# Where the gate of a convolution module is computed: GpSimd and ScalarE before, one VectorE pass in the middle of another chunk's taps after

## The chip, the cores and the metric

The kernel runs on one core of a Trainium2 chip. The metric is the device time of one execution in microseconds (us), lower is better. Engines are named as the profile names them: PE (TensorE, the matmuls; PEld its weight loads), DVE (VectorE), ACT (ScalarE), POOL (GpSimd) and SP (SyncE, which here only issues DMAs).

## What is computed

The reference is a two-layer backbone over 1024 latent and 256 context tokens of width 1024. Layer 0 mixes tokens with a Conformer convolution module, layer 1 with a gated linear attention; each is followed by a mixture of experts. The change touches one step of layer 0's convolution module:

```python
def conv_module(h, pw1_w, pw1_b, dw_w, dw_b, ln_g, ln_b, pw2_w, pw2_b):
    a, g = jnp.split(h @ pw1_w + pw1_b, 2, axis=-1)
    u = a * jax.nn.sigmoid(g)
    u = lax.conv_general_dilated(u, dw_w[:, None, :], ...) + dw_b   # 31 taps per channel
    u = jax.nn.silu(layernorm(u, ln_g, ln_b))
    return u @ pw2_w + pw2_b
```

## The kernel before

The program runs stage after stage, with a barrier of all engines between two. The stage in question is `conv_taps`. It holds the normalised input transposed (`ht`, channels on partitions, in two fp32r halves `hi` and `lo`, so that one fp32 product is three matmuls, lines 98 to 100) and works on eight chunks of 128 output channels; chunk number 2i + b uses buffer b of the pair i. In this document the chunks are counted 0 to 7. Per chunk:

- SP loads the chunk's weights (`raw`, line 427); ACT rounds them to `w.hi` (`high`, line 563); POOL computes the rest, `w.lo` (`low`, line 469, 128x2048). `w` is a single buffer, so `high` waits until the previous chunk's products are done.
- PE computes the two halves of pw1, `za` (for a) and `zg` (for g), in three groups of columns of 256, 512 and 512 (`CONV_GROUPS`: the context tokens, then the latent ones), a group at a time. There is one PSUM buffer for each group of each half, so PE's next chunk waits, group by group, until the last one was read.
- Behind each chunk PE computes some columns of the modulation vectors (`units`, line 541): three units behind a chunk of buffer 0, two behind one of buffer 1. Their weights come by DMA (line 438), ACT takes the sum (line 574), POOL adds the bias (line 490, 2x512) and stores it by DMA (line 493).
- The gate u = (za + bias) * sigmoid(zg + bias): ACT writes sg = sigmoid (line 587) and copies za + bias to `u` in SBUF (line 589), POOL multiplies `u` by `sg` in place (line 477), one operation for each group and engine.
- DVE computes the 31 taps over 1295 columns: two `tensor_scalar` (lines 631 and 633) and 29 `scalar_tensor_tensor` (line 638), alternately into `acc[0]` and `acc[1]`, then their sum (line 642), after a small copy of the next chunk's per-channel scalars (line 613). It waits for the three `u_ready` of its chunk before the first tap.

The order on each engine is written out by hand and every queue is in order. The lines that make the waits around the gate are these, PE's before each group and ACT's before its chunk:

```python
516                     for g, (t0, n, _) in enumerate(CONV_GROUPS):
518                         if not (first and b == 0):
519                             pe.wait_ge(s(f"a_ready{g}{1 - b}"), i + b)
```

POOL's order is low, units' output, gate for each chunk. The stage ends when DVE's last sum is done; then the barrier and the stage of the second product (`pw_...` in the profile) follow.

Of the kernel before, what the change touches and what calls it, by code (L numbers as in the profile page):

```python
# [385 lines left out]
ADA_UNITS = [(0, 0, 2, 0, 2 * D), (0, 0, 2, 1, 2 * D), (0, 1, 3, 0, 0), (1, 1, 3, 1, 0), (1, 1, 3, 2, 0)]  # L386


def conv_taps(nc, d, ht, vt, vecs, cs):

    with ExitStack() as ctx:
# [20 lines left out]
        with nc.Block() as block:  # L414
# [47 lines left out]
            @block.gpsimd  # L462
            def _(pool):
                for b in range(2):
                    pool.memset(u[b][:, :], 0.0).then_inc(s("u_zero"), 1)

                def low(b, i):
                    pool.wait_ge(s(f"w_hi{b}"), i + 1)
                    pool.tensor_tensor(w.lo[:, :, :, :], raw[b][:, :, :, :], w.hi[:, :, :, :].bitcast(F32),
                                       ALU.subtract).then_inc(s(f"w_lo{b}"), 1)  # L470

                def gate(b, i):

                    for g, (t0, n, c0) in enumerate(CONV_GROUPS):
                        pool.wait_ge(s(f"sig_ready{g}{b}"), i + 1)
                        pool.wait_ge(s(f"a_ready{g}{b}"), i + 1)
                        pool.tensor_tensor(u[b][:, c0:c0 + n], u[b][:, c0:c0 + n], sg[g][:, 0:n], ALU.mult)\
                            .then_inc(s(f"u_ready{g}{b}"), 1)

                def units_out(b, i, first):  # L480

                    for j, (when, l, per, at, c0) in enumerate(ADA_UNITS):
                        if when != b:
                            continue
                        u = i * len(ADA_UNITS) + j
                        pool.wait_ge(s("ada_b_loaded"), (u + 1) * 16)
                        pool.wait_ge(s("ada_taken"), u + 1)
                        if not (first and j == 0):
                            pool.wait_ge(s("stored"), u * 16)
                        pool.tensor_tensor(ada_row[:, :], ada_sum[:, :], ada_b[:, :], ALU.add)\  # L490
                            .then_inc(s("ada_out"), 1)
                        pool.wait_ge(s("ada_out"), u + 1)
                        pool.dma_start(d.mods[l].rearrange("s m n -> s (m n)")[:, ds((i * per + at) * N + c0, N)],
                                       ada_row[:, :]).then_inc(s("stored"), 16)

                low(0, 0)
                gate(0, 0)
                low(1, 0)
                units_out(0, 0, True)
                gate(1, 0)  # L500
                with pool.Fori(1, pairs) as i:
                    low(0, i)
                    units_out(1, i - 1, False)
                    gate(0, i)
                    low(1, i)
                    units_out(0, i, False)
                    gate(1, i)
                units_out(1, pairs - 1, False)
                pool.wait_ge(s("stored"), 16 * pairs * len(ADA_UNITS))

            @block.tensor
            def _(pe):
                pe.wait_ge(s("rows_loaded"), 96)
                for k in range(KC):
                    last = pe.transpose(pv[:, k, :], rows[:, k * P:(k + 1) * P], ident[0:VEC_ROWS, 0:VEC_ROWS])
                last.then_inc(s("pv_ready"), 1)

                def chunk(b, i, first):
                    pe.wait_ge(s(f"w_lo{b}"), i + 1)
                    for g, (t0, n, _) in enumerate(CONV_GROUPS):  # L520

                        if not (first and b == 0):
                            pe.wait_ge(s(f"a_ready{g}{1 - b}"), i + b)
                        for h, z in ((1, zg[g]), (0, za[g])):
                            for k in range(KC):
                                last = product3(pe, z[:, 0:n], w.hi[:, k, h, :], w.lo[:, k, h, :],
                                                ht.hi[:, k, t0:t0 + n], ht.lo[:, k, t0:t0 + n], k == 0, k == KC - 1)
                        last.then_inc(s(f"z_ready{g}{b}"), 1)

                def units(b, i, first):  # L530
                    for j, unit in enumerate(ADA_UNITS):
                        if unit[0] != b:
                            continue
                        u = i * len(ADA_UNITS) + j
                        if not (first and j == 0):

                            pe.wait_ge(s("ada_taken"), u)
                        for h in range(2):
                            pe.wait_ge(s(f"ada_loaded{h}"), (u + 1) * 16)
                            for k in range(KC // 2):  # L540
                                last = pe.matmul(ada_acc[0:2, :], cs[:, h * (KC // 2) + k, :], ada_w[h][:, k, :],  # L541
                                                 start=h == 0 and k == 0, stop=h == 1 and k == KC // 2 - 1)
                            last.then_inc(s(f"ada_used{h}"), 1)

                for b in range(2):
                    chunk(b, 0, True)
                    units(b, 0, True)
                with pe.Fori(1, pairs) as i:
                    for b in range(2):
                        chunk(b, i, False)  # L550
                        units(b, i, False)

            @block.scalar
            def _(act):
                act.preload_act_table(ACT.Sigmoid)
                act.wait_ge(s("u_zero"), 2)

                def high(b, i, first):
                    act.wait_ge(s(f"w_loaded{b}"), i * 32 + 32)
# [16 lines left out]
                def chunk(b, i, first):  # L576

                    act.wait_ge(s(f"vec_ready{b}"), i + 1)
                    if not first:

                        act.wait_ge(s("taps_summed"), i * 2 + (b - 1))
                    for g, (t0, n, c0) in enumerate(CONV_GROUPS):
                        act.wait_ge(s(f"z_ready{g}{b}"), i + 1)
                        if not (first and b == 0):

                            act.wait_ge(s(f"u_ready{g}{1 - b}"), i + b)
                        act.activation(sg[g][:, 0:n], zg[g][:, 0:n], ACT.Sigmoid, bias=vec[b][:, V_BG:V_BG + 1])\
                            .then_inc(s(f"sig_ready{g}{b}"), 1)
                        act.activation(u[b][:, c0:c0 + n], za[g][:, 0:n], ACT.Identity, bias=vec[b][:, V_BA:V_BA + 1])\
                            .then_inc(s(f"a_ready{g}{b}"), 1)  # L590

                high(0, 0, True)
                chunk(0, 0, True)
# [13 lines left out]
            def _(dve):  # L607
# [4 lines left out]
                def vector(b, i):  # L612
                    dve.tensor_copy(vec[b][:, :], vecs[:, ds(i * 2 + b, 1), :].rearrange("p o v -> p (o v)"))\
                        .then_inc(s(f"vec_ready{b}"), 1)

                def chunk(b, i, first=False, last=False):
                    n = i + 1

                    if b == 0:
                        vector(1, i)  # L620
                    elif not last:
                        vector(0, i + 1)
                    dve.wait_ge(s(f"vec_ready{b}"), n)
                    for g in range(3):
                        dve.wait_ge(s(f"u_ready{g}{b}"), n)
                    if not (first and b == 0):

                        dve.wait_ge(s("taps_summed"), i * 2 + b)


                    dve.tensor_scalar(acc[0][:, :], u[b][:, 0:CONV_OUT], vec[b][:, 0:1], vec[b][:, V_DWB:V_DWB + 1],
                                      ALU.mult, ALU.add).then_inc(s(f"tap0{b}"), 1)
                    dve.tensor_scalar(acc[1][:, :], u[b][:, 1:1 + CONV_OUT], vec[b][:, 1:2], None, ALU.mult)\
                        .then_inc(s(f"tap1{b}"), 1)
                    for k in range(2, TAPS):
                        q = k % 2
                        dve.wait_ge(s(f"tap{q}{b}"), i * len(range(q, TAPS, 2)) + k // 2)
                        dve.scalar_tensor_tensor(acc[q][:, :], u[b][:, k:k + CONV_OUT], vec[b][:, k:k + 1],  # L638
                                                 acc[q][:, :], ALU.mult, ALU.add).then_inc(s(f"tap{q}{b}"), 1)
                    for q in range(2):  # L640
                        dve.wait_ge(s(f"tap{q}{b}"), n * len(range(q, TAPS, 2)))
                    dve.tensor_tensor(vt[:, ds(i * 2 + b, 1), :].rearrange("p o n -> p (o n)"), acc[0][:, :],
                                      acc[1][:, :], ALU.add).then_inc(s("taps_summed"), 1)

                vector(0, 0)
                for b in range(2):
                    chunk(b, 0, first=True)
                with dve.Fori(1, pairs - 1) as i:
# [1895 lines left out]
```

## Time and profile before

| | us |
|---|---|
| median of 3 runs | 3388.13 |
| lowest and highest | 3384.37, 3390.13 |
| the profiled execution | 3385.44 |
| its span in the trace | 3383.8 |
| DVE, PE, ACT, POOL busy in the whole span | 2113.4, 2720.6, 1407.5, 509.8 |
| the taps stage, first load to last sum | about 118 to 605 |

The whole-program shares mix stages with different limits: PE is the busiest engine over the span, but in the stage that is changed another engine is. The stage has therefore to be read by itself, with the windows that are cut at its own borders, and then the timelines of the engines in it, which list instructions in order of time with the idle time in front of them and what ended it.

### The profile page before, as it was taken

To read this page: it belongs to the slowest core of one execution; us is meant where nothing else is said; L and a number is where in the kernel's file an instruction comes from. 1 tells how busy PE (TensorE), PEld (TensorE's weight loads), DVE (VectorE), ACT (ScalarE), POOL (GpSimd) and SP (SyncE) were. 2 spreads that over 40 slices of the span, in tenths; PEclk is the share of its full clock that TensorE was granted. 3 is DMA by queue.
4 is the path that set the end of the run, shared out by engine and by line. 5 is a ranking of instruction groups with operands and counts; after the bars stand their busy time and mean duration, and the time that the engine had idled before them with its cause. 6 is when DMAs were issued, how large, how long until landed. Compare 5 with 4: busy or idle time off the path is not lost. (4 is left out here: it accounts for less than half of the span.)

```text
span 3383.8 us, 39400 instructions
## 1 busy us (share of the span) xinstructions
PE 2720.6 (80%) x12298; PEld 2063.0 (61%) x12298; DVE 2113.4 (62%) x1769; ACT 1407.5 (42%) x1439; POOL 509.8 (15%) x432
## 2 busy tenths in 40 slices
PE   4598994595399999999925998989775399999980
PEld 1454552484278888888824886766464278888860
DVE  2399999455476777588444002346464488888865
ACT  1211110443166666577323113323232177777752
POOL 0136331100001010011051000022100010110104
PEclk7699997796599999999956999979887599999995
DMA  8243440224188988799564111022354299999965
GB/s 296 90 150 100 137 137 25 94 75 171 48 312 319 332 322 320 276 364 389 210 247 148 72 47 45 13 77 94 111 219 153 100 372 389 390 385 388 395 264 214
DMA packets 296869, 701.09 MB, mean 207 GB/s; under 512 B 22000, under 2 KB 49136, under 8 KB 296774
## 3 DMA queue, kind: packets, MB, share of 16 engines
q1 hardware_dynamic: 256538, 562.40, 46.4%
q0 software_dynamic: 24320, 83.98, 7.0%
q10 hardware_dynamic: 15936, 53.75, 4.2%
q8 instruction: 42, 0.69, 0.1%
q14 instruction: 33, 0.27, 0.0%
HBM read 610.05 MB, written 91.06 MB: 207 GB/s over the span
## 5 line engine op out<-in xcount | busy, mean ns | idle before, releaser
L1379 DVE TENSOR_TENSOR moe_w_lo<-moe_w_raw,moe_w_hi 128x2048 fp32r<-128x2048 f32 x384 | 862.0, 2286 | 83.8 <-ACT moe_w_hi L1308 47.3
L1308 ACT ACTIVATE moe_w_hi<-moe_w_raw 128x2048 fp32r<-128x2048 f32 x384 | 714.0, 1908 | 57.0 <-issue 36.7
L638 DVE SCALAR_TENSOR_TENSOR taps_acc<-taps_u,taps_vec,taps_acc 128x1295 f32<-128x1295 f32 x232 | 382.9, 1725 | 0.0
L98 PE MATMUL moe_pg<-moe_w_hi,moe_xt_hi 128*128 128x512 f32 x592 | 243.7, 412 | 11.3 <-DVE moe_xt_lo L1390 5.9
L98 PE MATMUL moe_py<-moe_w_hi,moe_at_hi 128*128 128x512 f32 x592 | 241.7, 408 | 11.9 <-DVE moe_w_lo L1379 8.2
L99 PE MATMUL moe_pg<-moe_w_lo,moe_xt_hi 128*128 128x512 f32 x592 | 236.9, 400 | 0.0
L100 PE MATMUL moe_pg<-moe_w_hi,moe_xt_lo 128*128 128x512 f32 x592 | 236.9, 400 | 0.0
L99 PE MATMUL moe_py<-moe_w_lo,moe_at_hi 128*128 128x512 f32 x592 | 235.2, 397 | 0.0
L100 PE MATMUL moe_py<-moe_w_hi,moe_at_lo 128*128 128x512 f32 x592 | 234.7, 396 | 0.0
L100 PE MATMUL moe_pu<-moe_w_hi,moe_xt_lo 128*128 128x512 f32 x592 | 234.3, 396 | 0.0
L98 PE MATMUL moe_pu<-moe_w_hi,moe_xt_hi 128*128 128x512 f32 x592 | 234.1, 396 | 0.0
L99 PE MATMUL moe_pu<-moe_w_lo,moe_xt_hi 128*128 128x512 f32 x592 | 234.1, 396 | 0.0
L1211 POOL COPY moe_idx<-plan_token 128x1 int32 (+1 forms) x76 | 16.0, 210 | 1074.5 <-PE moe_pxt L1249 1074.3
L541 PE MATMUL taps_ada_acc<-taps_ada_w,silu_c 128*2 128x512 f32 x320 | 150.2, 625 | 33.1 <-DMA taps_ada_w<-in_ada_w 33.1
L1425 DVE TENSOR_TENSOR moe_a<-moe_sil,moe_pu 128x512 f32<-128x512 f32 x74 | 50.9, 688 | 180.8 <-issue 114.3
L364 PE MATMUL norm_pt<-norm_ident,norm_h 128*128 128x128 f32 x224 | 55.1, 427 | 119.1 <-DVE norm_h L334 119.1
L1318 ACT ACTIVATE moe_y<-moe_py 128x1024 f32<-128x1024 f32 x74 | 76.0, 1027 | 147.7 <-PE moe_py L100 147.7
L98 PEld LDWEIGHTS moe_pg<-moe_w_hi,moe_xt_hi 128*128 128x128 f32 x592 | 113.5, 192 | 36.4 <-issue 12.5
L1217 POOL DMA_INDIRECT moe_xg<-scratch_experts_in,moe_idx x76 | 116.1, 1527 | 124.4 <-issue 124.4
L2197 DVE SCALAR_TENSOR_TENSOR scan_state<-scan_state,scan_es,scan_pds 128x256 f32<-128x256 f32 x160 | 67.4, 477 | 107.2 <-issue 68.6
L98 PEld LDWEIGHTS moe_py<-moe_w_hi,moe_at_hi 128*128 128x128 f32 x592 | 112.1, 189 | 35.8 <-issue 12.3
L1333 ACT ACTIVATE moe_xt_hi<-moe_pxt 128x1024 fp32r<-128x1024 f32 x74 | 75.9, 1025 | 134.6 <-PE moe_pxt L1249 134.6
(296 smaller groups left out, 5544.1 us busy)
## 6 DMA issues: line engine op xcount, KB each, us to landing
moe_w_raw<-in_moe_w SPq DMA_DIRECT2D x384, 1024.0 KB, 10.3
taps_ada_w<-in_ada_w SPq DMA_DIRECT2D x40, 1024.0 KB, 5.3
scratch_experts_out<-moe_y ACTq DMA_DIRECT2D x57, 512.0 KB, 6.3
norm_x<-scratch_residual SPq DMA_DIRECT2D x28, 512.0 KB, 3.5
scan_v<-scratch_gla_values SPq DMA_DIRECT2D x20, 512.0 KB, 4.6
scratch_experts_in<-norm_h POOLq DMA_DIRECT2D x18, 512.0 KB, 3.3
comb_x<-scratch_residual SPq DMA_DIRECT2D x18, 512.0 KB, 5.5
ada_w<-in_ada_w SPq DMA_DIRECT2D x4, 2048.0 KB, 28.6
```

The costliest lines, as they stand in the source:

```text
L98: pe.matmul(out, xh, wh, start=start, stop=False)
L99: pe.matmul(out, xh, wl, start=False, stop=False)
L100: return pe.matmul(out, xl, wh, start=False, stop=stop)
L364: last = pe.transpose(pt[b][:, k, :], h[b][:, k * P:(k + 1) * P], ident[:, :])
L541: last = pe.matmul(ada_acc[0:2, :], cs[:, h * (KC // 2) + k, :], ada_w[h][:, k, :], start=h == 0 and k == 0, stop=h == 1 and k == KC // 2 - 1)
L638: dve.scalar_tensor_tensor(acc[q][:, :], u[b][:, k:k + CONV_OUT], vec[b][:, k:k + 1], acc[q][:, :], ALU.mult, ALU.add).then_inc(s(f"tap{q} ...
L1217: pool.indirect_dma_start(xg[0:rows, :], None, d.hd[:, :], bass.IndirectOffsetOnAxis(idx[0:rows, :], 0))\
L1308: act.activation(hi[m][:, cut, :], raw[m][p][:, cut, :], ACT.Copy).then_inc(s(f"{m}_hi{h}"), 1)
L1318: act.activation(y[:, :], py[:, :], ACT.Copy).then_inc(s("y_out"), 1)
L1333: act.activation(xt_hi[:, :, :], pxt[:, :, :], ACT.Copy).then_inc(s("xt_hi"), 1)
L1379: dve.tensor_tensor(lo[m][:, cut, :], raw[m][p][:, cut, :], hi[m][:, cut, :].bitcast(F32), ALU.subtract).then_inc(s(f"{m}_lo{h}"), 1)
L2197: last = dve.scalar_tensor_tensor(state[r][:, h, :], state[r][:, h, :], es[r][st.b][:, h, end:end + 1], pds[:, h, :], ALU.mult, ALU.add)
```

## The change

ACT's copy of za to `u` and POOL's product are removed. In their place DVE does one `scalar_tensor_tensor` for each group, (za + bias) * sg, that reads za from PSUM and sg from SBUF and writes `u`. DVE does chunk 0's gate before its first tap. The gate of every later chunk stands between tap 15 and tap 16 of the chunk before it (`GATE_AT = 16`). PE's wait for `a_ready` becomes a wait for `sig_ready` and `u_ready`; ACT's waits for `taps_summed` and for the zeroed `u` go, and the latter is now DVE's.

```diff
+GATE_AT = 16
...
             @block.gpsimd
...
-                def gate(b, i):
-
-                    for g, (t0, n, c0) in enumerate(CONV_GROUPS):
-                        pool.wait_ge(s(f"sig_ready{g}{b}"), i + 1)
-                        pool.wait_ge(s(f"a_ready{g}{b}"), i + 1)
-                        pool.tensor_tensor(u[b][:, c0:c0 + n], u[b][:, c0:c0 + n], sg[g][:, 0:n], ALU.mult)\
-                            .then_inc(s(f"u_ready{g}{b}"), 1)
...
             @block.tensor
...
-                            pe.wait_ge(s(f"a_ready{g}{1 - b}"), i + b)
+                            pe.wait_ge(s(f"sig_ready{g}{1 - b}"), i + b)
+                            pe.wait_ge(s(f"u_ready{g}{1 - b}"), i + b)
...
             @block.scalar
-                act.wait_ge(s("u_zero"), 2)
...
-                    if not first:
-
-                        act.wait_ge(s("taps_summed"), i * 2 + (b - 1))
...
-                        act.activation(u[b][:, c0:c0 + n], za[g][:, 0:n], ACT.Identity, bias=vec[b][:, V_BA:V_BA + 1])\
-                            .then_inc(s(f"a_ready{g}{b}"), 1)
...
             @block.vector
+                def gate(b, i):
+
+                    for g, (t0, n, c0) in enumerate(CONV_GROUPS):
+                        dve.wait_ge(s(f"z_ready{g}{b}"), i + 1)
+                        dve.wait_ge(s(f"sig_ready{g}{b}"), i + 1)
+                        dve.scalar_tensor_tensor(u[b][:, c0:c0 + n], za[g][:, 0:n], vec[b][:, V_BA:V_BA + 1],
+                                                 sg[g][:, 0:n], ALU.add, ALU.mult).then_inc(s(f"u_ready{g}{b}"), 1)
...
                     for k in range(2, TAPS):
                         q = k % 2
+                        if k == GATE_AT:
+                            if b == 0:
+                                dve.wait_ge(s("vec_ready1"), n)
+                                gate(1, i)
+                            elif not last:
+                                dve.wait_ge(s("vec_ready0"), n + 1)
+                                gate(0, i + 1)
...
                 vector(0, 0)
+                dve.wait_ge(s("u_zero"), 2)
+                dve.wait_ge(s("vec_ready0"), 1)
+                gate(0, 0)
```

On DVE, from the stage's first copy to the first chunk's sum (names: `taps_u` is u, `taps_za` the PSUM tile of a, `taps_sg` the sigmoid):

```order
-L609 COPY channel_vectors<-taps_pv 128x288
-L613 COPY taps_vec<-channel_vectors 128x36 x2
-L631 TENSOR_SCALAR taps_acc<-taps_u,taps_vec 128x1295
-L633 TENSOR_SCALAR taps_acc<-taps_u,taps_vec 128x1295
-L638 SCALAR_TENSOR_TENSOR taps_acc<-taps_u,taps_vec,taps_acc 128x1295 x29
...
+L607 SCALAR_TENSOR_TENSOR taps_u<-taps_za,taps_vec,taps_sg 128x256
+L607 SCALAR_TENSOR_TENSOR taps_u<-taps_za,taps_vec,taps_sg 128x512 x2
+L599 COPY taps_vec<-channel_vectors 128x36
+L624 TENSOR_SCALAR taps_acc<-taps_u,taps_vec 128x1295
+L626 TENSOR_SCALAR taps_acc<-taps_u,taps_vec 128x1295
+L638 SCALAR_TENSOR_TENSOR taps_acc<-taps_u,taps_vec,taps_acc 128x1295 x14
+L607 SCALAR_TENSOR_TENSOR taps_u<-taps_za,taps_vec,taps_sg 128x256
+L607 SCALAR_TENSOR_TENSOR taps_u<-taps_za,taps_vec,taps_sg 128x512 x2
+L638 SCALAR_TENSOR_TENSOR taps_acc<-taps_u,taps_vec,taps_acc 128x1295 x15
```

The unbroken run of 29 taps is now one of 14 and one of 15, with the three operations of the next chunk's gate between them; this form stands in chunks 0 to 6, and chunk 7 keeps the 29 in a row.

On POOL, from the zeroing of u to the output of the first units:

```order
-L465 MEMSET taps_u 128x1325 x2
-L469 ISA
-L469 TENSOR_TENSOR taps_w_lo<-taps_raw,taps_w_hi 128x2048
-L477 TENSOR_TENSOR taps_u<-taps_u,taps_sg 128x256
-L477 TENSOR_TENSOR taps_u<-taps_u,taps_sg 128x512 x2
-L469 TENSOR_TENSOR taps_w_lo<-taps_raw,taps_w_hi 128x2048
...
+L468 MEMSET taps_u 128x1325 x2
+L472 ISA
+L472 TENSOR_TENSOR taps_w_lo<-taps_raw,taps_w_hi 128x2048 x2
+L485 TENSOR_TENSOR taps_ada_row<-taps_ada_sum,taps_ada_b 2x512
+L488 DMA scratch_modulation<-taps_ada_row 2x512
```

The three products between the two `low` are gone, and so at each later chunk; the order of what is left is the same.

## Rows read from the trace of the kernel before

**Rows 1.** Busy time by stage: window, length, then the columns of the first line.

```profile
core 0: us, PE busy (x) PEld busy (x) DVE busy (x) ACT busy (x) POOL busy (x), PEclk, DMA share, GB/s
...
170.00:605.00 435.00, 341.06 (x1322) 191.70 (x1320) 432.85 (x262) 46.52 (x69) 152.14 (x68) 0.90 0.33 107
```

**Rows 2.** The same view, cut into DVE's eight chunks: the last one, and the sum.

```profile
558.50:604.70 46.20, 0.00 (x0) 0.00 (x0) 46.09 (x32) 0.00 (x0) 0.00 (x0) 0.50 0.00 0
sum 434.70, PE 341.06 PEld 191.70 DVE 432.85 ACT 46.52 POOL 152.14; mean PE 42.63 PEld 23.96 DVE 54.11 ACT 5.82 POOL 19.02
```

**Rows 3.** DVE's timeline (start, us [idle before]); last, the tap's line, ns min/median/max.

```profile
169.94 0.95 DVE L631 TENSOR_SCALAR taps_acc<-taps_u,taps_vec 128x1295 f32<-128x1295 f32 x1 [39.89 <-POOL taps_u L477]
170.81 5.13 DVE L633 TENSOR_SCALAR taps_acc<-taps_u,taps_vec 128x1295 f32<-128x1295 f32 x1
175.86 47.22 DVE L638 SCALAR_TENSOR_TENSOR taps_acc<-taps_u,taps_vec,taps_acc 128x1295 f32<-128x1295 f32 x29
...
225.81 4.91 DVE L631 TENSOR_SCALAR taps_acc<-taps_u,taps_vec 128x1295 f32<-128x1295 f32 x1 [0.20 <-POOL taps_u L477]
...
560.14 42.94 DVE L638 SCALAR_TENSOR_TENSOR taps_acc<-taps_u,taps_vec,taps_acc 128x1295 f32<-128x1295 f32 x29
...
L638 DVE SCALAR_TENSOR_TENSOR taps_acc<-taps_u,taps_vec,taps_acc x232: 1552/1556/5800, 175.9 to 601.5; 128x1295 f32<-128x1295 f32 x116
```

**Rows 4.** DVE's and POOL's timelines, single operations; then POOL's three lines, ns min/median/max.

```profile
435.18 5.80 DVE L638 SCALAR_TENSOR_TENSOR taps_acc<-taps_u,taps_vec,taps_acc 128x1295 f32<-128x1295 f32 x1
433.85 5.76 POOL L469 TENSOR_TENSOR taps_w_lo<-taps_raw,taps_w_hi 128x2048 fp32r<-128x2048 f32 x1
184.26 2.56 DVE L638 SCALAR_TENSOR_TENSOR taps_acc<-taps_u,taps_vec,taps_acc 128x1295 f32<-128x1295 f32 x1
213.29 2.39 DVE L638 SCALAR_TENSOR_TENSOR taps_acc<-taps_u,taps_vec,taps_acc 128x1295 f32<-128x1295 f32 x1
202.56 1.94 DVE L638 SCALAR_TENSOR_TENSOR taps_acc<-taps_u,taps_vec,taps_acc 128x1295 f32<-128x1295 f32 x1
256.24 21.53 POOL L477 TENSOR_TENSOR taps_u<-taps_u,taps_sg 128x512 f32<-128x512 f32 x1 [10.35 <-ACT taps_u L589]
...
L469 POOL TENSOR_TENSOR taps_w_lo<-taps_raw,taps_w_hi x8: 4492/4654/5758, 133.6 to 477.1; 128x2048 fp32r<-128x2048 f32 x8
...
L490 POOL TENSOR_TENSOR taps_ada_row<-taps_ada_sum,taps_ada_b x20: 1277/2057/2623, 175.2 to 544.9; 2x512 f32<-2x512 f32 x20
...
L477 POOL TENSOR_TENSOR taps_u<-taps_u,taps_sg x24: 639/1492/21532, 146.6 to 529.7; 128x512 f32<-128x512 f32 x16, 128x256 f32<-128x256 f32 x8
```

**Rows 5.** The timelines of ACT, POOL and PE up to chunk 1's last sigmoid.

```profile
167.30 0.69 ACT L587 ACTIVATE taps_sg<-taps_zg,taps_vec 128x512 f32<-128x512 f32 x1 [9.61 <-PE taps_za L100]
167.88 0.68 ACT L589 ACTIVATE taps_u<-taps_za,taps_vec 128x512 f32<-128x512 f32 x1
...
168.70 1.09 POOL L477 TENSOR_TENSOR taps_u<-taps_u,taps_sg 128x512 f32<-128x512 f32 x1 [9.79 <-ACT taps_u L589]
...
167.19 7.03 PE L541 MATMUL taps_ada_acc<-taps_ada_w,silu_c 128*2 128x512 f32 x16
...
185.41 8.72 PE L541 MATMUL taps_ada_acc<-taps_ada_w,silu_c 128*2 128x512 f32 x16 [2.00 <-DMA taps_ada_w<-in_ada_w]
...
221.91 0.69 ACT L587 ACTIVATE taps_sg<-taps_zg,taps_vec 128x512 f32<-128x512 f32 x1 [9.61 <-PE taps_za L100]
```

**Rows 6.** Two DVE lines with an input in PSUM, elsewhere: ns min/median/max.

```profile
L2197 DVE SCALAR_TENSOR_TENSOR scan_state<-scan_state,scan_es,scan_pds x160: 473/476/484, 2226.1 to 2431.7; 128x256 f32<-128x256 f32 x160
...
L1425 DVE TENSOR_TENSOR moe_a<-moe_sil,moe_pu x74: 686/689/690, 948.6 to 3273.0; 128x512 f32<-128x512 f32 x74
```

**Rows 7.** PE's products of chunks 1 and 2, as windows in the columns of rows 1.

```profile
194.06:221.80 27.74, 27.74 (x145) 23.70 (x144) 27.74 (x19) 2.70 (x5) 6.33 (x4) 1.00 0.15 53
238.20:265.50 27.30, 27.30 (x144) 23.36 (x142) 27.30 (x19) 2.47 (x5) 13.08 (x4) 1.00 0.18 65
```

**Rows 8.** PE's timeline: the last of the three units behind chunk 2.

```profile
292.29 9.95 PE L541 MATMUL taps_ada_acc<-taps_ada_w,silu_c 128*2 128x512 f32 x16 [10.50 <-DMA taps_ada_w<-in_ada_w]
```

## The prediction and its working

> **What bounds the kernel now.** The stage borders come first: the windows cut at them show DVE busy 432.85 of 435.00 us between its first tap and the end of the taps stage, PE 341.06, POOL 152.14 and ACT 46.52 [rows 1]. So between 170 and 605 us the kernel goes at DVE's pace, though DVE is far from the busiest engine over the whole program. A barrier follows, so what the stage's end moves by, the program's end moves by; nothing in the later stages is edited.
>
> Next, what one chunk costs DVE. The window of the last chunk, in which POOL does nothing, is 46.2 us; eight of these would be 369.6, while the eight windows sum to 434.7 [rows 2]. The missing 65.1 us are DVE instructions made longer by POOL. A tap alone records 1.556 us, and the 29 undisturbed ones of the last chunk take 42.94, so from start to start it is (42.94 - 1.556) / 28 = 1.478 [rows 3]. Beside POOL's `low` one takes 5.80, beside a bias addition 2.56, beside a 512-column product 2.39 and beside the 256-column one 1.94 [rows 4]. Less 1.556 that is 4.24, 1.00, 0.83 and 0.38 us for each. Of the 65.1, the seven `low` behind the first of eight take 28.8 (three of them hit a `tensor_scalar`: 4.91 against 0.95, 3.96 each [rows 3, 4]) and the twenty bias additions 20.2, which leaves about 16.1 for the gate's 21 products, their stray hits on small operations and the 0.2 us waits in front of a chunk. Counting three products per chunk for seven chunks gives 7 x (0.38 + 2 x 0.83) = 14.3. I take 16.1 and keep 14.3 as the low end.
>
> **The start of the stage.** Before, chunk 0's last gate goes ACT sigmoid to 167.99, ACT copy to 168.56, POOL product to 169.79, first tap at 169.94 [rows 5]. After, DVE reads PSUM itself at about 168.1, beside nothing else, for one operation of 0.69 [rows 6], and the first tap is at about 168.85: **-1.1 us**.
>
> **The gates on DVE.** One gate is three operations with one input in PSUM. The nearest rows are 0.476 us for 256 columns and 0.689 for 512 [rows 6]; less the 0.078 by which records overlap on DVE (1.556 against 1.478), that is 0.40 + 2 x 0.61 = 1.62 us, at most 1.85 with no overlap. I take 1.65, nearest to the back-to-back taps around it. It can't be below the lower figure, since the same operations end no sooner anywhere in the trace. Six gates (chunks 2 to 7) come to **+9.9** (9.7 to 11.1); chunk 0's is in the start above, chunk 1's in the next step. The Trainium skill, "VectorE: DVE Perf Modes", section on the TRN2 errata, gives 120 cycles plus the columns for a PSUM source, 0.39 and 0.66 us here: 1.71 a gate, 10.3 for six, so the sum would grow by 0.4; the trace's records are 0.03 to 0.08 longer than the page's figures.
>
> **The wait in chunk 0.** This is the step that decides. DVE's queue is in order, so the gate of chunk 1, which stands before tap 16 of chunk 0, holds back fifteen taps until PE has made chunk 1's products. When does DVE get there? The 29 taps start at 175.86; fourteen of them at 1.478, plus three bias additions at 1.0 (POOL's `low` has been paid already in the 5.13 of line 633 [rows 3]), reach 199.6; with the earlier start 198.5. When is the gate ready? PE starts chunk 1 at 194.06, directly behind the units, which wait for weights by DMA [rows 5, 7], so nothing that the change frees can start it sooner; its products take 27.7 us [rows 7], ACT's last sigmoid is 221.91 to 222.60 [rows 5]. The last gate operation then runs from 222.7 and tap 16 starts at 223.3. **+24.8 us** between 198.5 and 223.3, of which 1.6 are chunk 1's gate and some 23 idle; the first two groups are done inside that time. Before, DVE waited 0.20 us in front of chunk 1, at 225.81 [rows 3]. The products of chunk 1 had all of chunk 0's taps to hide under, and now have half of them.
>
> **Do later gates wait too?** From tap 16 at 223.3 DVE needs 23.8 us to the end of chunk 0, plus one `low` and two bias additions (6.2): chunk 1's first tap at 253.3. It then costs 46.2 + 1.65 + 4.2 + 2.5 = 54.6 us a chunk on average, and a gate stands 22.4 us plus POOL's hits after a chunk's start. Gate 2 comes at 281 or so; PE's products for it end as now at 265.5 [rows 7]. Three units take 26.9 us where nothing holds them (167.19 to 194.1 [rows 5]), so chunk 3's products run from about 292.5 to 320, and its gate is reached at about 335. Chunk 4's: PE waits for gate 3 (u_ready, about 337), ends 364, gate at 390. From there PE waits for DVE and not the reverse; the smallest margin is 15 us.  So later gates don't wait.
>
> **The sum.** -1.1 (start) + 24.8 (chunk 0's wait and gate 1) + 9.9 (six gates) - 16.1 (POOL's products gone from DVE's way) = **+17.5 us**. Removing ACT's copies (24 at up to 0.68) gives nothing beyond the start: ACT is busy a ninth of the stage. Against the profiled execution's 3385.44 us (span 3383.8, 1.6 lie around it) that gives 3402.9; the median of the three runs lies 2.7 above the profiled one, so the forecast is 3388.1 + 17.5 = 3405.6, or **3406 us**. With the low end for POOL's products and the high end for the gates it is +20.5; with the wait shorter by 2 us, +15.5.
>
> **Rivals.** (1) POOL is held out and PE comes late. One product of POOL's started at 256.24 and took 21.53 us, though an undisturbed one takes 1.09 [rows 4, 5]: DVE's taps passed it one after another until the chunk's end. If a `low` is held like that, its chunk's products begin late; with a margin of 15 us at gate 3 a hold of 21 costs a second stall of about 6 and saves 4.2 of DVE's, a few such make +3 to +12: 3409 to 3418. It did so once before: while POOL was held at 256 to 280, PE's units fell behind, with 10.50 us idle before the last of them [rows 8]. Against it: in the whole stage none of the seven `low` and none of the twenty bias additions was held beyond one tap (their longest records are 5.76 and 2.62 [rows 4]). The Trainium skill, "SBUF — State Buffer", section "Who interferes with whom", calls the port pair that the two share an exclusive lock that whoever starts first holds for its whole instruction, the other waiting. The 5.80 against 5.76 agree, the 21.53 doesn't, since there POOL lost to one tap after another; by the rule alone this rival is nil and the sum stays.
> (2) The other side: faster, because POOL's remaining work falls out of DVE's way. What is left of contention is six `low` (25) and seventeen bias additions (17), 42 us. If DVE, now with fewer interruptions, keeps POOL out as at 256.24 until a gate, whose operations read only one input from SBUF, these costs vanish; beyond 17.5 us saved, that is four `low` and one addition, the kernel is no longer slower, and at most it ends at 3388 + 17.5 - 42 = 3364. The mechanism exists, since DVE's taps beside the product at 256.24 were not stretched; but it has not once struck a `low`.
> (3) The wait isn't there: chunk 1's products start before 194 because POOL's queue is lighter. Then the sum is -1.1 + 1.6 + 9.9 - 16.1 = -5.7, or 3382. For this the units before them would have to end earlier, and their last releaser is a DMA [rows 5], issued after PE frees the buffer. They would have to end 23 us earlier, and nothing in these rows can give that.
> (4) The change does not do what it says: the gate from PSUM runs much slower beside matmuls. At twice the price, 3.3 a gate, it is +10 more: 3416. The row with 74 executions, 686 to 690 ns, stands beside running matmuls [rows 6].
>
> **How the numbers follow.** The forecast has 0.80, rival (1) 0.08, (2) 0.04, (3) 0.02, (4) 0.03, and 0.03 for what I don't see. A difference of 0.2% (6.8 us) is what a measurement of this kernel can tell from none. Slower by more: forecast, (1), (4) and most of the rest, 0.92; within: 0.04, from the mild forms of (2) and (3); faster: 0.04. The range takes the forecast's +15.5 to +20.5, 3 us of the medians' own scatter at either side and the nearer part of (1) and (4): 3398 to 3417.
>
> **What would show it.** In the trace of the changed kernel DVE should idle some 10 us before each of the two 512-column gates of chunk 1 and a little before the 256-column one, 23 in all, released by ACT's sigmoid or PE's za, and nowhere else; the 512-column gates should record about 0.69 us; chunk 7's taps should take 42.94 again; the stage should end at about 622 where it ended at 604.6; ACT should be free of copies and POOL of products, and POOL should stretch DVE's instructions by some 49 us rather than 65 (7 of these ahead of chunk 0's wait, which they only shorten). The forecast is wrong if DVE idles at a later gate, if a `low` records over 10 us, or if the stage is right and later stages moved.

## The result, and the profile after

| | before | after |
|---|---|---|
| median, us (6 runs each) | 3388.33 | 3403.32 |
| lowest and highest | 3384.37, 3390.7 | 3401.92, 3406.23 |
| span of the profiled execution | 3383.8 | 3403.0 |
| taps stage: DVE's first tap to its last sum | 169.94 to 604.63 | 169.86 to 616.94 |

The change makes the kernel slower: the ratio is 1.0046, with a 95% interval from 1.0033 to 1.0059. Of the 15 us, 12.3 are the taps stage, which ends so much later; from the first tap to the last sum it lasts 447.1 us for 434.7. Two windows cut at its borders answer to [rows 1, 2] (columns: window, length, PE, PEld, DVE, ACT and POOL busy, granted clock, DMA):

```profile
169.86:616.94 447.08, 341.05 (x1325) 191.53 (x1323) 423.52 (x283) 36.07 (x48) 134.79 (x47) 0.89 0.31 104
616.94:3403.00 2786.06, 2296.89 (x10674) 1824.95 (x10674) 1627.22 (x1442) 1327.39 (x1318) 341.95 (x353) 0.89 0.61 223
```

DVE was idle for 2 us of the stage before; now it is idle for 23.6. Its timeline says where. It answers to [rows 3]; in brackets stands the idle time ahead of an operation and what ended it.

```profile
169.86 0.95 DVE L624 TENSOR_SCALAR taps_acc<-taps_u,taps_vec 128x1295 f32<-128x1295 f32 x1
170.73 5.20 DVE L626 TENSOR_SCALAR taps_acc<-taps_u,taps_vec 128x1295 f32<-128x1295 f32 x1
175.84 23.91 DVE L638 SCALAR_TENSOR_TENSOR taps_acc<-taps_u,taps_vec,taps_acc 128x1295 f32<-128x1295 f32 x14
201.29 0.48 DVE L607 SCALAR_TENSOR_TENSOR taps_u<-taps_za,taps_vec,taps_sg 128x256 f32<-128x256 f32 x1 [1.54 <-ACT taps_sg L575]
212.34 0.75 DVE L607 SCALAR_TENSOR_TENSOR taps_u<-taps_za,taps_vec,taps_sg 128x512 f32<-128x512 f32 x1 [10.56 <-ACT taps_sg L575]
223.21 0.75 DVE L607 SCALAR_TENSOR_TENSOR taps_u<-taps_za,taps_vec,taps_sg 128x512 f32<-128x512 f32 x1 [10.13 <-ACT taps_sg L575]
223.88 28.55 DVE L638 SCALAR_TENSOR_TENSOR taps_acc<-taps_u,taps_vec,taps_acc 128x1295 f32<-128x1295 f32 x15
...
276.48 1.80 DVE L607 SCALAR_TENSOR_TENSOR taps_u<-taps_za,taps_vec,taps_sg 128x256 f32<-128x256 f32 x3
278.19 27.86 DVE L638 SCALAR_TENSOR_TENSOR taps_acc<-taps_u,taps_vec,taps_acc 128x1295 f32<-128x1295 f32 x15
...
572.46 42.94 DVE L638 SCALAR_TENSOR_TENSOR taps_acc<-taps_u,taps_vec,taps_acc 128x1295 f32<-128x1295 f32 x29
615.43 1.51 DVE L642 TENSOR_TENSOR taps_out<-taps_acc 128x1295 f32<-128x1295 f32 x1
```

The fourteen taps end at 199.75, and then DVE waits three times for ACT's sigmoid of chunk 1: 1.54, 10.56 and 10.13, or 22.2 us. No later gate waits: at 276.48 the three operations follow each other, in 1.71 us from the start of the first to the start of the next tap.

On POOL something else changed. These rows answer to [rows 4], where the longest `low` (then line 469, now 472) was 5.76 and the longest bias addition (then 490, now 485) 2.62:

```profile
268.66 12.27 POOL L472 TENSOR_TENSOR taps_w_lo<-taps_raw,taps_w_hi 128x2048 fp32r<-128x2048 f32 x1 [26.76 <-ACT taps_w_hi L554]
...
328.75 5.80 POOL L472 TENSOR_TENSOR taps_w_lo<-taps_raw,taps_w_hi 128x2048 fp32r<-128x2048 f32 x1 [25.83 <-ACT taps_w_hi L554]
...
478.84 15.08 POOL L472 TENSOR_TENSOR taps_w_lo<-taps_raw,taps_w_hi 128x2048 fp32r<-128x2048 f32 x1 [27.11 <-ACT taps_w_hi L554]
...
546.12 22.14 POOL L485 TENSOR_TENSOR taps_ada_row<-taps_ada_sum,taps_ada_b 2x512 f32<-2x512 f32 x1 [31.70 <-ACT taps_ada_sum L565]
```

A `low` that takes 4.5 us alone is on record for 12 and 15 here; such an operation, which waits on record while DVE's taps pass it, is called held below. The first one ends at 280.93, 2.7 us into the first tap behind the gate, and that tap shows what it cost DVE:

```profile
278.19 4.11 DVE L638 SCALAR_TENSOR_TENSOR taps_acc<-taps_u,taps_vec,taps_acc 128x1295 f32<-128x1295 f32 x1
```

4.11 less 1.56 is 2.55 us, where a `low` before stretched its tap by 4.24.

### The profile page after: what moved, and what is told of

Same layout as the page of the kernel before. It is cut to its first block and busy times, and to the rows that moved or that the text cites. A ratio compares the mean times of both kernels' runs of the same rounds, so it can differ in the third digit from the quotient of the medians.

```text
span 3403.0 us, 39388 instructions
## 1 busy us (share of the span) xinstructions
PE 2721.8 (80%) x12298; PEld 2065.2 (61%) x12298; DVE 2106.0 (62%) x1793; ACT 1396.1 (41%) x1415; POOL 483.8 (14%) x408
## 5 line engine op out<-in xcount | busy, mean ns | idle before, releaser
L98 PE MATMUL moe_pg<-moe_w_hi,moe_xt_hi 128*128 128x512 f32 x592 | 243.7, 412 | 11.4 <-DVE moe_xt_lo L1393 6.2
L98 PEld LDWEIGHTS moe_py<-moe_w_hi,moe_at_hi 128*128 128x128 f32 x592 | 112.2, 190 | 35.8 <-issue 12.3
L98 PE MATMUL glav_acc<-glav_w_hi,ht_next_hi 128*128 128x512 f32 x288 | 115.5, 401 | 19.5 <-DVE glav_w_lo L1754 19.5
L100 PEld LDWEIGHTS moe_pg<-moe_w_hi,moe_xt_lo 128*128 128x128 f32 x592 | 113.2, 191 | 27.4
```

The source lines that it names most:

```text
L98: pe.matmul(out, xh, wh, start=start, stop=False)
L100: return pe.matmul(out, xl, wh, start=False, stop=stop)
```

## The experiments

**Question 1: is the loss chunk 0's wait, and does it go by the gate's place?** Three kernels move `GATE_AT`, and one moves only chunk 0's gate. Each edit up to question 3 is against the changed kernel.

```diff
-GATE_AT = 16
+GATE_AT = 30
```

> The changed kernel with every gate in front of the last tap (tap 30) instead of tap 16. Theory A (the loss is the wait in chunk 0, and its size is the distance between the gate's place and PE's products): fourteen more taps of 1.478 us run before the wait, so the 22.2 us that DVE idled shrink to 2 or 3, chunk 0 ends some 20.7 us earlier, later gates find their products ready, and the taps stage ends at 596 us where the changed kernel has 616.9; the time is 3382 to 3385, some 0.15% faster than the kernel before. Rival B (the place only moves the wait to another gate, since PE can't keep up with an earlier DVE): DVE idles again at gates 2 and 3, the stage ends no earlier than 606, the time is 3392 or more. Rival C (POOL's work is held out for longer, up to 25 us, PE's units fall behind): idle at gates 4 to 7, stage end 600 to 610.

Measured: 3382.01 us, ratio to the kernel before 0.9979 (0.997 to 0.9988); the stage ends at 599.17. DVE waits 0.32 us before chunk 1's last gate operation and nowhere else but 2.31 at gate 5:

```profile
222.26 0.75 DVE L607 SCALAR_TENSOR_TENSOR taps_u<-taps_za,taps_vec,taps_sg 128x512 f32<-128x512 f32 x1 [0.32 <-ACT taps_sg L575]
...
435.95 1.95 DVE L607 SCALAR_TENSOR_TENSOR taps_u<-taps_za,taps_vec,taps_sg 128x256 f32<-128x256 f32 x3 [2.31 <-ACT taps_sg L575]
```

The same pass from PSUM, put where its data is ready, turns 0.46% slower into 0.21% faster than the kernel before. Theory A holds for the size of the loss; rival B is out. C shows in the trace: two bias additions were on record for 36.91 and 36.66 us, and gate 5 waited 2.31 us behind the second. ACT's queue has its next sum of units ahead of chunk 5's sigmoid, and that sum stood until the addition ended at 434.79; the addition for its part got in only when DVE stood still at the gate, from 433.6 on, for want of this sigmoid.

```diff
-GATE_AT = 16
+GATE_AT = 8
```

> The changed kernel with every gate in front of tap 8 instead of tap 16. Theory A: eight taps fewer run before the wait, which grows by 8 x 1.478 = 11.8 us; later gates keep a margin of some 3 us or more. Stage end 628.7, time 3415 (0.8% over the kernel before). If DVE's idle time is given back later the time stays near 3403.

Measured: 3418.37 us, ratio 1.0083 (1.0068 to 1.0099); first tap to last sum 466.1 us against 447.1, so 19.0 more and not 11.8. The idle time at chunk 1's gate grew to 15.62 + 10.56 + 10.13 = 36.3. The rest is `low`: its longest record is 5.58 here, none was held, and each stretched its tap in full, by 4.24 us where five of the changed kernel's took 2.55. So 14.1 more idle, five times 1.69 more for `low`, and 3.5 less for the bias additions (they stretched DVE by 16.9 us in sum, and by 20.4 in the changed kernel) make 19.1 for the 19.0:

```profile
269.71 5.80 DVE L638 SCALAR_TENSOR_TENSOR taps_acc<-taps_u,taps_vec,taps_acc 128x1295 f32<-128x1295 f32 x1
```

```diff
-GATE_AT = 16
+GATE_AT = 24
```

> The changed kernel with every gate in front of tap 24. Theory A: eight more taps ahead of chunk 0's wait, which shrinks by 11.8 us to 10 or so; stage end 605, time 3391. With the held POOL work of theory H a `low` that arrives behind its gate can be held for over 20 us and make PE late, as in the kernel with only chunk 0's gate moved: then 3 to 8 us more, 3394 to 3399.

Measured: 3392.37 us, ratio 1.0006 (0.9997 to 1.0015), first tap to last sum 435.7, 11.4 less than with tap 16 (11.8 expected). `low` was held five times, as at tap 16, but always ahead of its gate, so PE was not late.

```diff
-                        if k == GATE_AT:
+                        if k == (30 if first and b == 0 else GATE_AT):
```

> The changed kernel with the gate in chunk 0 alone in front of tap 30; all others stay in front of tap 16. Theory A: the wait in chunk 0 shrinks to 2 or 3 us and chunk 1 starts 20.7 us earlier, at 233.4 (254.1 in the changed kernel), but its gate at tap 16 is then reached at about 258, where PE's products of chunk 2 end at 266.5: a second wait of some 9 us. The stage ends at 605 to 606, the time is 3392. If the loss were not the wait but the gates' own price or POOL's, nothing would change: 3403.

Measured: 3407.43 us, ratio 1.0044 (1.003 to 1.0058): a miss for theory A. Chunk 1 did start at 231.5 and its gate did wait, for 10.1 us. But then two `low` were held for 26 us, because they reached POOL's front just behind a gate and not ahead of it, and PE stood still for them:

```profile
322.58 26.09 POOL L472 TENSOR_TENSOR taps_w_lo<-taps_raw,taps_w_hi 128x2048 fp32r<-128x2048 f32 x1 [26.45 <-ACT taps_w_hi L554]
```

and in the view of PE's waits (us in total, times, longest):

```profile
PE taps_zg L98 <- POOL taps_w_lo L472: 25.4, 2, 12.7
```

DVE then idled 3.44 and 4.25 us more at the gates of chunks 4 and 6. That is 7.7 of the 14 us by which the stage ended later than expected (620.1). The expectation also took over the changed kernel's price of `low`: here each of the seven stretched DVE by 3.96 to 4.31 us, 29.2 in sum for 21.3, which is 7.9 more. This is the first rival of the prediction, in another kernel. Of the six executions one took 3394.04 us, near the 3392 expected, one 3401.69, and four 3406.64 to 3410.29: in this kernel a small shift decides whether a `low` comes ahead of a gate or behind it. That this is what separates the six is argued, since only one of them has a trace.

**Question 2: why did `low` cost 2.55 us and not 4.24?** In the changed kernel the held `low` may have done its first 1.7 us beside the gate, whose operations read one input from PSUM. The next kernel gives the gate two SBUF inputs. With ACT's copy come back its waits (for the zeroed `u` and for the sum of the taps that last read it) and PE's wait for `a_ready` in place of `u_ready`.

```diff
+                        act.activation(u[b][:, c0:c0 + n], za[g][:, 0:n], ACT.Identity, bias=vec[b][:, V_BA:V_BA + 1])\
+                            .then_inc(s(f"a_ready{g}{b}"), 1)
...
-                        dve.scalar_tensor_tensor(u[b][:, c0:c0 + n], za[g][:, 0:n], vec[b][:, V_BA:V_BA + 1],
-                                                 sg[g][:, 0:n], ALU.add, ALU.mult).then_inc(s(f"u_ready{g}{b}"), 1)
+                        dve.wait_ge(s(f"a_ready{g}{b}"), i + 1)
+                        dve.tensor_tensor(u[b][:, c0:c0 + n], u[b][:, c0:c0 + n], sg[g][:, 0:n], ALU.mult)\
+                            .then_inc(s(f"u_ready{g}{b}"), 1)
```

> The gate stays on DVE at tap 16, but its operations read two inputs from SBUF: ACT copies za + bias to u as in the kernel before, and DVE multiplies u by sg in place. Theory D (five of the changed kernel's seven `low` records started their work beside the gates, since these leave the second read path free, which is why they stretched DVE by 2.55 us and not 4.24): now a held `low` finds no such place, either it is held on until DVE drains in front of a chunk's sum (records up to 36 us, PE's next products late, DVE idle at later gates), or it enters at the gate's first wait and costs its whole 4.2 us. Stage end 8 us or more later than 616.9. Rival E (the input's place does not matter, what lets POOL in is the change of instruction at the gate): `low` gets in at the gate all the same at 2.55 us, stage end 617 +- 2.

Measured: 3410.23 us, ratio 1.0059 (1.0043 to 1.0074); first tap to last sum 454.8, 7.7 more than the changed kernel. Both theories had half of it. `low` enters at the gate all the same (E), but behind it and not beside it, at full price (D):

```profile
279.59 1.62 DVE L614 TENSOR_TENSOR taps_u<-taps_u,taps_sg 128x256 f32<-128x256 f32 x3
...
281.13 5.80 DVE L645 SCALAR_TENSOR_TENSOR taps_acc<-taps_u,taps_vec,taps_acc 128x1295 f32<-128x1295 f32 x1
...
271.58 13.98 POOL L472 TENSOR_TENSOR taps_w_lo<-taps_raw,taps_w_hi 128x2048 fp32r<-128x2048 f32 x1 [26.57 <-ACT taps_w_hi L555]
```

5.80 - 4.11 = 1.69 us on each of five taps is 8.5 of stage time, about the 7.7 measured, with gates that are 0.17 shorter (1.54 from start to start against 1.71). So a DVE operation with an input in PSUM leaves room for POOL to work beside it, and for a held `low` that is worth as much as the gate costs. The edit also changes the kind of operation, but a tap is of the same kind as the changed kernel's gate, with two SBUF inputs, and is stretched. A kernel of question 4 shows it a second way: in the rows below, DVE's and POOL's of the kernel with `low` on DVE and the gates at tap 16, a whole bias addition runs beside a gate that takes its usual 1.79 us, and nothing is stretched.

```profile
271.39 1.79 DVE L598 SCALAR_TENSOR_TENSOR taps_u<-taps_za,taps_vec,taps_sg 128x256 f32<-128x256 f32 x3
...
271.51 1.26 POOL L480 TENSOR_TENSOR taps_ada_row<-taps_ada_sum,taps_ada_b 2x512 f32<-2x512 f32 x1 [31.74 <-ACT taps_ada_sum L556]
```

The Trainium skill, "SBUF — State Buffer", section "Who interferes with whom", says that a DVE instruction with at most one SBUF input, outside the two-port modes, does not contend with GpSimd; by these kernels the trace agrees.

**Question 3: what keeps POOL out?** Here every fifth tap also waits for the one right before it, so that DVE runs dry there.

```diff
                         dve.wait_ge(s(f"tap{q}{b}"), i * len(range(q, TAPS, 2)) + k // 2)
+                        if k % 5 == 0:
+                            dve.wait_ge(s(f"tap{1 - q}{b}"), i * len(range(1 - q, TAPS, 2)) + (k + 1) // 2)
```

> The changed kernel, but each fifth tap (5, 10, 15, 20, 25, 30) also waits for the tap just before it, so that DVE runs dry for some 0.2 us there. Theory H (POOL is kept out as long as DVE's taps follow each other without a gap, and enters at the first gap or change of instruction): no POOL record is longer than five taps plus its own work, some 12 us for a `low` and 10 for a bias addition, where the changed kernel has 12.27, 14.87, 15.08 and 22.14; `low` enters in front of the gate more often and then costs 4.24 us and not 2.55. Six gaps of 0.2 us in eight chunks are 8 to 10 us, so the stage lasts 455 to 463 us from the first tap instead of 447, the time is 3412 to 3420. Rival P (it hangs on the phase at which POOL arrives within a tap, not on the run of taps): records over 12 us stay.

Measured: 3415.73 us, ratio 1.0077 (1.0062 to 1.0091); first tap to last sum 462.4. POOL was never held (line, then ns min/median/max):

```profile
L485 POOL TENSOR_TENSOR taps_ada_row<-taps_ada_sum,taps_ada_b x20: 1251/1879/2517, 175.6 to 552.4; 2x512 f32<-2x512 f32 x20
...
L472 POOL TENSOR_TENSOR taps_w_lo<-taps_raw,taps_w_hi x8: 4495/5100/5865, 133.2 to 484.2; 128x2048 fp32r<-128x2048 f32 x8
```

The changed kernel had 22143 and 15084 as the longest. Theory H holds and P falls: it is the unbroken run of taps that keeps POOL out. The time lies in the expected range, but not by the gaps alone that its sum named: of the 15.3 us more, the 48 gaps take some 5.5 (1.593 us from start to start in place of 1.478, so 0.12 each and not 0.2), and `low` at its full price takes 8.4 (29.7 for 21.3). In the changed kernel holding cost DVE nothing; it let `low` start beside the gates.

**Question 4: what is it worth to take `low` off POOL altogether?** The edit moves it to DVE, behind the gate (chunk 0's in front of everything); first with the gates at tap 30.

```diff
-                def low(b, i):
-                    pool.wait_ge(s(f"w_hi{b}"), i + 1)
-                    pool.tensor_tensor(w.lo[:, :, :, :], raw[b][:, :, :, :], w.hi[:, :, :, :].bitcast(F32),
-                                       ALU.subtract).then_inc(s(f"w_lo{b}"), 1)
...
+                def low(b, i):
+                    dve.wait_ge(s(f"w_hi{b}"), i + 1)
+                    dve.tensor_tensor(w.lo[:, :, :, :], raw[b][:, :, :, :], w.hi[:, :, :, :].bitcast(F32),
+                                      ALU.subtract).then_inc(s(f"w_lo{b}"), 1)
...
+                        if k == 4 and first and b == 0:
+                            low(1, 0)
                         if k == GATE_AT:
                             if b == 0:
                                 dve.wait_ge(s("vec_ready1"), n)
                                 gate(1, i)
+                                if not last:
+                                    low(0, i + 1)
                             elif not last:
                                 dve.wait_ge(s("vec_ready0"), n + 1)
                                 gate(0, i + 1)
+                                low(1, i + 1)
```

> Every gate in front of tap 30, and `low` (the 128x2048 subtraction) moved from POOL to DVE, right behind the gate of the chunk before; chunk 1's stands in front of tap 4 of chunk 0. Theory: on DVE it costs 2.2 us (2.29 by the record of the same operation in the expert stage) where POOL's cost DVE 2.55 to 4.24 and could be held. Six of the seven in the taps: 6 x 2.2 = 13 for about 22, and chunk 0's `low` in front of everything takes 2.3 for POOL's 4.5, so all starts 2 us sooner. Stage end 588 to 592 (599.2 in the kernel with all gates at tap 30), time 3371 to 3376. Rival: PE's chunk now waits for DVE's gate place for its w.lo too and DVE idles at later gates: 3380 or more.

Measured: 3373.7 us, ratio 0.996 (0.9947 to 0.9973), stage end 585.9: the fastest kernel of this study, 15 us faster than before. A `low` on DVE takes 2.29:

```profile
274.66 2.29 DVE L603 TENSOR_TENSOR taps_w_lo<-taps_raw,taps_w_hi 128x2048 fp32r<-128x2048 f32 x1
```

The rival does not show: DVE idles at no gate behind chunk 0. Two bias additions are still held, for 34.8 us each; nothing waits for them long enough to reach DVE. Against this kernel, the next one moves only the gates:

```diff
-GATE_AT = 30
+GATE_AT = 16
```

> `low` on DVE behind each gate as in low_dve30, but the gates in front of tap 16 as in the changed kernel. Theory: the wait in chunk 0 is back; it is a matter of the gate's place alone. Against low_dve30 the first tap to the last sum takes 418.7 + 18 to 20 us, stage end 604 to 606, time 3392. Against the changed kernel the six `low` cost 13 us instead of 17 (4.25 and five of 2.55) and everything starts 2 us sooner: 6 us less, which gives 611, time 3397. Both can't hold; the difference shows whether held `low` is worth as much as the trace's 1.7 us for each.

Measured: 3392.77 us, ratio 1.0009 (1.0 to 1.0018), stage end 604.61, first tap to last sum 437.2. The first sum was right (418.7 + 18.5). The gate's place costs the stage 18.5 us here and 18.2 where POOL does the `low` (447.1 against 428.9). The second was 6 us off: to take `low` off POOL gains more than its stretches of single taps. The rest is in the bias additions: five of the twenty ran wholly beside a gate and stretched nothing, and all together stretched DVE by 14.8 us where they had stretched it by 20.4. Of the five that were held here, for 8.6 to 19.8 us, only one is among those; the other four each stretched a chunk's sum by 0.8 to 1.0 us.

**Question 5: do the later stages lose anything?** Behind the taps stage the first pair of profiles has 2779.17 and 2786.06 us for the same work.

> The kernel before, unchanged, as a second profile of it and a null comparison: from the end of the taps stage to the end the first profile has 2779.2 us, the changed kernel's 2786.1 and the kernels with moved gates 2782 to 2787, for the same work. If that part scatters from run to run, this profile lands anywhere in 2779 to 2787; if the change costs later stages something, it stays near 2779. Time 3388, ratio 1.000 +- 0.001.

> The changed kernel, unchanged: time 3403 if the taps stage's 12.3 us and a scatter of some us make up the difference, and the same pattern of held POOL work as in its first profile (`low` 12.3, 5.8, 14.9, 6.1 and 15.1 us) if this is set by the program and not by chance. If the later stages lose nothing, the ratio over many rounds comes down towards 1.0036 (12.3 us).

Measured: the kernel before again 3387.55 us, ratio 0.9997 (0.9988 to 1.0006); the changed kernel again 3403.86, ratio 1.0042 (1.0028 to 1.0056). Behind the stage:

```profile
605.87:3384.60 2778.73, 2293.18 (x10674) 1822.78 (x10674) 1627.49 (x1442) 1326.93 (x1318) 347.88 (x353) 0.89 0.61 224
616.85:3402.20 2785.35, 2294.97 (x10674) 1824.31 (x10674) 1627.26 (x1442) 1326.63 (x1318) 342.57 (x353) 0.89 0.61 223
```

The stage again differs by 12.2 us from the first tap to the last sum (447.15 and 434.96 us). The later part lasts 6.6 to 6.9 us longer in both profiles of the changed kernel, while the eight kernels with other edits have 2782.0 to 2787.0 there, faster ones included. The expectation of pure scatter is not borne out. A part of it, 1.3 us, is PE's clock, not work. In the scan stage eight matmuls that took 1.89 us take 3.18, in windows of 20 and 21.4 us around them whose granted clock is 0.81 and 0.72, means over stretches at 2.4 and at 1.2 GHz. A row of PE's timeline and a window of the kernel before, and then the same of the changed kernel:

```profile
2258.69 1.89 PE L2080 MATMUL scan_po<-scan_v,scan_att 128*128 128x256 f32 x8
```

```profile
2250.00:2270.00 20.00, 19.08 (x98) 13.12 (x96) 10.36 (x23) 5.34 (x10) 2.54 (x2) 0.81 0.16 53
```

```profile
2274.07 3.18 PE L2083 MATMUL scan_po<-scan_v,scan_att 128*128 128x256 f32 x8
```

```profile
2264.60:2286.00 21.40, 20.48 (x97) 14.34 (x96) 10.06 (x23) 5.34 (x10) 2.55 (x2) 0.72 0.15 50
```

In the second profiles the same eight matmuls take 1.89 and 3.09. Why the stretch at 1.2 GHz reaches them in one kernel and not in the other, and where the other 5.6 us come from, stays open; the medians ask for only 15.0 - 12.3 = 2.7 us from outside the stage. The pattern of held work is the program's, not chance, in the changed kernel: its second profile has `low` at 12.41, 5.64, 14.68, 6.16 and 15.28 us and an addition at 22.03. The kernel before held two of its gate products the second time too, but others, for 12.65 and 24.53 us where it had been 21.53 and 12.75.

## Why the prediction was right, and where it was off

- **What bounds the kernel.** Right. The stage's end moved by 12.3 us and the program's median by 15.0. The forecast was 3406, the measured median 3403.32, inside the range. Some luck is in how near it came: for the stage itself the forecast of 17.5 was 5.2 too high, and the part behind the stage, taken as unmoved, gave 2.7 of that back in the medians.
- **The start.** Forecast -1.1. From the start of ACT's last sigmoid of chunk 0 to the first tap it was 167.30 to 169.94 and is 168.17 to 169.86: 2.64 and 1.69, so -0.95. The first tap itself moved by 0.08 only, as that sigmoid came 0.87 us later: from 138 to 148 us, in chunk 0's products, the mean granted clock was 0.84 before and 0.73 after. In the second profiles (0.75 and 0.73) the first tap is at 170.91 and 169.70.
- **The wait in chunk 0.** Forecast 24.8 between DVE's arrival at tap 16 and its start; measured 199.75 to 223.88, 24.1, of which 22.2 idle for "some 23". The moved gates confirm it as the cause: 36.3 us idle with tap 8, 22.2 with 16 and 0.3 in chunk 1's gate with 30.
- **The gates on DVE.** Forecast 1.65 each, measured 1.71, six of them 10.3 for 9.9. A 512-column one is on record at 0.75 and not 0.69, the row of a two-input operation that I used [rows 6]; the Trainium skill's price in "VectorE: DVE Perf Modes", section on the TRN2 errata, from which 1.71 had been worked out as an estimate, gives the measured figure here.
- **POOL's products gone.** Forecast -16.1, low end -14.3. All that POOL saves DVE is what closes the balance: 24.1 + 10.3 - 12.4 (447.1 - 434.7) = 22.0. Of it `low` gives 7.5: seven cost 28.8 before, and now 4.3, 4.25 and five times 2.55, or 21.3. The bias additions give nothing (20.2 before, 20.4 after). That leaves 14.5 for the products and the small waits in front of the chunks; the stretches beside the products sum to 14.3, so the low end, counted from three products a chunk, was the better value.
- **What `low` costs afterwards.** This is the step that was mis-sized: "It then costs 46.2 + 1.65 + 4.2 + 2.5 = 54.6 us a chunk". I priced each remaining `low` at 4.2, as if only its own length mattered, and so put its part in the sum at nothing. Measured it is 2.55 for five of six, as it was held until a gate and worked beside it. The chunks 1 to 5 took 53.6, 52.8, 53.7, 52.8 and 53.7 us and not 54.6. Rival (2) named the mechanism and gave it 0.04 in its full form, where all contention vanishes; it came in a mild form and gave back 7.5 us, too little to change the sign. The evidence against it was read wrongly: the prediction said that no `low` had been held before. It had not, most likely since POOL's own gate products broke DVE's run of taps every 11 us, and it was these that the change removed; the count in the last section supports that, but no kernel tried it alone.
- **Do later gates wait?** Right: none did. The margin hung on the order, though: the `low` of 328.75 came up only 1.35 us ahead of the gate at 330.10. Where two of them came up behind a gate (chunk 0's gate at tap 30, the others at 16) PE was late and DVE waited at two more gates. Rival (1) is real, only not here.
- **Rivals (3) and (4)** did not occur: PE's chunk 1 ended at the same distance from chunk 0 within 0.4 us, and a 512-column gate operation takes 0.75 us beside running matmuls, not twice 0.69.
- **The later stages** were taken as unmoved. The profiles show 6.6 to 6.9 us there, the medians some 2.7; its cause is open.
- **The signs of being wrong.** Two of the three that the prediction named came true although the time was right: a `low` recorded over 10 us (12.27, 14.87 and 15.08), and later stages moved. The first tells of the mis-sized `low` above. It is no sign of a loss, as a held `low` cost DVE less and not more. POOL stretched DVE by 41.7 us in the stage (63.3 before), not by the 49 forecast.

## What to carry to other kernels

When work is moved onto an in-order engine as the next item's first step, the place in the current item is a deadline for the producer: put it where its data is ready in the first round too, since the pipeline is emptiest there. Here one number, tap 16 or tap 30, is the difference between 0.46% slower and 0.21% faster, for the same instructions. And an engine whose operations stretch another's is not only a cost per operation: taking away its small operations can change when its large ones get in.

## What the runs showed of the hardware

**POOL is kept out by a long unbroken run on DVE.** I counted, in the twelve profiles of this study, how many DVE operations had gone by, when a POOL operation of the stage came up, since DVE had last been stretched by POOL, had been idle or had done its `tensor_scalar` pair. With six or fewer, 296 of 301 POOL operations got in at once, mostly after the tap in progress. With seven or more, 31 of 51 were passed by at least two further taps, up to 15 of them; the other 20 came up at most two taps away from a gate, from a `low` on DVE or from a gap, and got in there. The count does not explain the five exceptions, and these include the longest records. The longest is this addition, 1.25 us when alone, in the kernel with all gates at tap 30; only four operations had gone by when it came up, and then 24 taps passed it:

```profile
344.72 36.91 POOL L485 TENSOR_TENSOR taps_ada_row<-taps_ada_sum,taps_ada_b 2x512 f32<-2x512 f32 x1 [7.64 <-ACT taps_ada_sum L565]
```

The Trainium skill calls what the two engines share an exclusive lock ("SBUF — State Buffer", "Who interferes with whom"). That fits a single meeting of two operations and agrees with the 5.80 us taps; it doesn't tell how long POOL is passed over here. The way out is a gap of 0.12 us in DVE's stream (the kernel with a drain at every fifth tap), a change of instruction, or an operation with an input in PSUM. Why some seven, and why the five exceptions, stays open.

**An operation of POOL cost DVE at most its own work, not its record.** A `low` on record for 15.08 us stretched DVE by 2.55, one of 5.57 by 4.24. The time to read is how much DVE's own operations exceed their undisturbed length.
